# First attention layer of a two-layer block: scores, turns and value products of two row tiles placed one behind the other, and a second buffer for turned probabilities

## The chip, the core and the metric

The program runs on one core of a Trainium2 chip. The core has TensorE for products (with a queue of its own for loading weights), VectorE, ScalarE and GpSimd for elementwise work, and SyncE, which here issues most transfers. The engines run their own instruction streams in order and meet at semaphores. The metric is the time of one execution on the device, in microseconds.

## The reference, cut to what matters

The whole program is a block of two attention layers on one sequence of 512 positions with 1024 features, then a second block (a recurrent branch, a sparse attention branch, a merge). The change is in the first attention layer alone:

```python
def mixer_a(hn, w_in, w_out, q_gain, k_gain, t5_bias):
    proj = hn @ w_in
    qkv = proj[..., :n_qkv].reshape(b, s, N_DIL_GROUPS, 3, N_HEADS, HEAD_DIM)
    gate = proj[..., n_qkv:]
    for g, (window, dilation) in enumerate(DILATED_PAIRS):       # 3 groups, 16 heads of 64
        q = rms_norm(qkv[:, :, g, 0], q_gain[g])
        k = rms_norm(qkv[:, :, g, 1], k_gain[g])
        v = qkv[:, :, g, 2]
        o, lse = dilated_group_attention(q, k, v, t5_bias[...], dilation, reach)
        outs.append(o)
        lses.append(lse)
    alpha = jax.nn.softmax(jnp.stack(lses), axis=0)
    y = jnp.sum(alpha[..., None] * jnp.stack(outs), axis=0)
    y = y.reshape(b, s, BRANCH_WIDTH) * jax.nn.silu(gate)
    return y @ w_out
```

## The kernel before

`dilated_attention` works on eight pairs of heads (p = 0 to 7). While the attention of pair p is computed, the projections of pair p + 1 are computed between its parts. A pair's projection has 13 units u: units 0 to 5 are q and k of the three groups, unit 6 the gate, unit 7 a value block in feature order, units 8 to 11 four value blocks of 256 columns, unit 12 the turning of unit 7 (four transposes). Each of the units 0 to 11 is 24 products: 8 slices of the features, each in three products of rounded high and low parts (`split_product`, lines 321 to 323). Units write two banks in turn, and unit n may start when VectorE has taken unit n - 2 (`project`, semaphore `s_pf`).

For a q or k unit the chain is: ScalarE squares it (1519) and rounds the square (1523); GpSimd forms the rounding's rest (1625); TensorE adds both up over the heads' features in `sum_squares` (1359, 1360), which stands inside the next unit behind 12 of its products; ScalarE makes the inverse norm by a logarithm and an exponential (`inv_norm`, 1507 and 1509); VectorE multiplies unit, gain and norm into `a_qk` (`take`, 1656). Behind the square, ScalarE rounds a block of weights for a later unit (1499) and GpSimd forms its rest (1612).

The attention of a pair has four row tiles t of 128 positions. S t: scores (1405), six or eight products with 64 rows in use; VectorE adds the bias and finds the peak in two passes for each head (`soft_peak`, 1700 and 1702); ScalarE takes four exponentials with their sums (`exps`, 1540); VectorE exchanges peaks and sums between the tiles of different order in eight small operations (`swap`, 1710 and 1711). C and D: shares of the groups. Then `normal` scales the tile's probabilities by the shares (1746), T t turns them on TensorE (1420) into the bank pair `ps_pt`, ScalarE copies one head and VectorE the other into `pt` (`keep_pt`, 1554 and 1754), and A t multiplies them with the values (1436). Behind A3 VectorE multiplies by the gate (`keep_y`, 1766).

The order of it all is written out by hand in two lists, which every engine's code walks through: `PERIOD` for the pairs 0 to 6 and `LAST` for pair 7, in which the out-projection's products (e, f, g, h) stand where the next pair's units do elsewhere. ScalarE and GpSimd do a unit's work at the unit's place; VectorE takes unit i - 1 at the place of unit i.

## Time and profile before

| | us |
|---|---|
| runs, median of 3 | 1609.79 |
| runs, lowest and highest | 1601.22, 1611.5 |
| span of the profiled execution | 1602.5 |
| TensorE busy in that span | 1536.9 (96%) |
| VectorE, ScalarE, GpSimd busy | 807.8, 772.9, 777.1 (50%, 48%, 48%) |
| the seven periods of `PERIOD`, 88 to 594.2 us | 506.2 |
| mean granted clock of TensorE, whole span | 0.987 |

A row of the timeline has the start in us, the duration in us, the engine, the line, the operation, out<-in by the program's names, the shape and a count of merged instructions; in brackets stands how long the engine was idle before, and who ended that. PE is TensorE, DVE VectorE, ACT ScalarE, POOL GpSimd. The matmul rows overlap, since products are pipelined: what a product costs is the distance between two starts, not its duration. A row of the busy times has the stretch, its length, busy us and number of instructions of PE, PEld (weight loading), DVE, ACT and POOL, then the granted clock of TensorE as a share of 2.4 GHz, the share of the transfer engines and GB/s. A row of the waits has who waited for whom: us in total, times, the longest.

### The profile page before, as it was taken

The page shows a single profiled execution, that of the slowest core. Times are in us where ns is not written, and L with a number is a line of the kernel's source. Part 1 is how long each engine was busy: PE and PEld are TensorE (multiplying, and loading weights), DVE is VectorE, ACT ScalarE, POOL GpSimd, SP SyncE. Part 2 cuts the span into 40 slices and gives each one's busy share as a digit, 9 for nine tenths or more (in the row PEclk, how much of TensorE's full clock was granted, in tenths as well). Part 3 has the DMA queues.
Part 4 walks back from the last instruction along what each step waited for, and adds up shares of the span by engine and source line. Part 5 has one row for each costly group of instructions (what it writes and reads, how often), then busy time and mean ns, then how long its engine had stood idle before and what let it go on. Part 6 is the DMA issues. An engine that isn't in the chain of part 4 may idle for free. (4 is left out here: it accounts for less than half of the span.)

```text
span 1602.5 us, 29989 instructions
## 1 busy us (share of the span) xinstructions
PE 1536.9 (96%) x11712; PEld 1236.3 (77%) x11712; DVE 807.8 (50%) x1933; ACT 772.9 (48%) x1558; POOL 777.1 (48%) x474
## 2 busy tenths in 40 slices
PE   7999999999999999999999999999987999999997
PEld 5888787878888787767777776677776886778886
DVE  5145455464545457434445324298437754274545
ACT  4654637364554644455666633356754432352322
POOL 3734436262534443366555544326747651475551
PEclk9999999999999999999999999999979999999998
DMA  6323132232413131355444215132000000323331
GB/s 153 105 83 109 53 97 81 82 97 66 121 40 109 53 96 53 79 153 155 139 140 124 66 54 159 40 73 66 15 29 3 4 17 29 105 80 97 95 98 53
DMA packets 239125, 131.00 MB, mean 82 GB/s; under 512 B 28646, under 2 KB 233518, under 8 KB 238968
## 3 DMA queue, kind: packets, MB, share of 16 engines
q1 hardware_dynamic: 231448, 114.09, 25.6%
q10 hardware_dynamic: 7536, 14.98, 3.1%
q8 instruction: 94, 1.54, 0.4%
q14 instruction: 47, 0.39, 0.1%
HBM read 126.62 MB, written 2.43 MB: 81 GB/s over the span
## 5 line engine op out<-in xcount | busy, mean ns | idle before, releaser
L1612 POOL TENSOR_TENSOR w_low<-a_w_raw,w_high 128x1024 fp32r<-128x1024 f32 x70 | 173.4, 2478 | 56.3 <-ACT w_high L1499 56.3
L321 PE MATMUL a_proj<-h_low,w_high 128*128 128x512 f32 x488 | 196.3, 402 | 1.2 <-POOL h_low L1630 1.2
L323 PE MATMUL a_proj<-h_high,w_high 128*128 128x512 f32 x488 | 192.0, 393 | 0.0
L322 PE MATMUL a_proj<-h_high,w_low 128*128 128x512 f32 x488 | 191.1, 392 | 0.0
L1625 POOL TENSOR_TENSOR a_sq_low<-a_sq,a_sq_high 128x512 fp32r<-128x512 f32 x48 | 63.0, 1312 | 249.9 <-ACT a_sq_high L1523 249.9
L907 POOL TENSOR_TENSOR w_low<-b_w_raw,w_high 128x1024 fp32r<-128x1024 f32 x40 | 100.4, 2512 | 97.1 <-ACT w_high L741 97.1
L321 PE MATMUL b_proj<-h_low,w_high 128*128 128x512 f32 x288 | 116.6, 405 | 1.4 <-POOL h_low L946 0.8
L323 PE MATMUL b_proj<-h_high,w_high 128*128 128x512 f32 x288 | 113.6, 394 | 0.0
L322 PE MATMUL b_proj<-h_high,w_low 128*128 128x512 f32 x288 | 113.5, 394 | 0.0
L321 PEld LDWEIGHTS a_proj<-h_low,w_high 128*128 128x128 f32 x488 | 91.7, 188 | 23.8 <-issue 1.4
L323 PEld LDWEIGHTS a_proj<-h_high,w_high 128*128 128x128 f32 x488 | 91.7, 188 | 20.7
L322 PEld LDWEIGHTS a_proj<-h_high,w_low 128*128 128x128 f32 x488 | 91.8, 188 | 19.0
L1540 ACT ACTIVATE a_probs<-a_probs,a_stat 128x256 f32<-128x256 f32 x128 | 63.2, 495 | 68.3 <-DVE a_stat L1702 68.3
L1499 ACT ACTIVATE w_high<-a_w_raw 128x1024 fp32r<-128x1024 f32 x70 | 73.3, 1047 | 40.5 <-PE a_proj L323 37.5
L1746 DVE TENSOR_SCALAR a_probs<-a_probs,a_share 128x256 f32<-128x256 f32 x128 | 90.4, 768 | 0.3
L1656 DVE SCALAR_TENSOR_TENSOR a_qk<-a_proj,a_gains,a_rn 128x128 f32<-128x128 f32 (+2 forms) x76 | 39.2, 559 | 86.5 <-ACT a_rn L1509 86.1
L3378 POOL TENSOR_TENSOR merge_w_low<-f_wt,merge_w_high 128x1024 fp32r<-128x1024 f32 x22 | 53.5, 2431 | 35.9 <-ACT merge_w_high L3322 35.9
L321 PE MATMUL a_proj<-a_wv_low,h_high 128*128 128x256 f32 x240 | 68.1, 284 | 0.0
L322 PE MATMUL a_proj<-a_wv_high,h_low 128*128 128x256 f32 x240 | 66.9, 279 | 0.0
L323 PE MATMUL a_proj<-a_wv_high,h_high 128*128 128x256 f32 x240 | 66.8, 279 | 0.0
L2328 POOL TENSOR_TENSOR w_low<-sparse_w_raw,w_high 128x1024 fp32r<-128x1024 f32 x15 | 35.8, 2386 | 60.9 <-ACT w_high L2245 58.5
L321 PEld LDWEIGHTS b_proj<-h_low,w_high 128*128 128x128 f32 x288 | 54.6, 190 | 13.4 <-issue 1.4
(554 smaller groups left out, 4187.0 us busy)
## 6 DMA issues: line engine op xcount, KB each, us to landing
a_w_raw<-in_a_w_in_dram SPq DMA_DIRECT2D x78, 512.0 KB, 3.7
b_w_raw<-in_b_w_in_dram SPq DMA_DIRECT2D x30, 512.0 KB, 4.1
b_ada_w<-in_ada_w_dram ACTq DMA_DIRECT2D x24, 512.0 KB, 3.7
f_wt<-in_w_in_dram SPq DMA_DIRECT2D x18, 512.0 KB, 3.6
sparse_w_raw<-in_w_in_dram SPq DMA_DIRECT2D x17, 512.0 KB, 3.6
a_bias<-scr_a SPq DMA_DIRECT2D x32, 128.0 KB
a_w_raw<-in_a_w_out_dram SPq DMA_DIRECT2D x8, 512.0 KB, 4.3
b_w_raw<-in_b_w_out_dram SPq DMA_DIRECT2D x8, 512.0 KB, 4.2
```

What stands on the lines that cost most here:

```text
L321: nc.tensor.matmul(out, lh, rl, start=first, stop=False)
L322: nc.tensor.matmul(out, ll, rh, start=False, stop=False)
L323: return nc.tensor.matmul(out, lh, rh, start=False, stop=last)
L907: nc.gpsimd.tensor_tensor(low(slot_of(b)), raw[:, n % RAW, :, :], high(slot_of(b)), ALU.subtract).then_inc(s_wl, 1)
L1499: nc.scalar.activation(high(slot_of(b)), raw[:, n % RAW, :, :], ACT.Copy).then_inc(s_wh, 1)
L1540: nc.scalar.activation(e, e, ACT.Exp, scale=-1.0, bias=stat[:, own, part, t, h, 0:1], accum_out=stat[:, own, part, t, h, 1:2]).then_inc(s_ ...
L1612: nc.gpsimd.tensor_tensor(low(slot_of(b)), raw[:, n % RAW, :, :], high(slot_of(b)), ALU.subtract).then_inc(s_wl, 1)
L1625: nc.gpsimd.tensor_tensor(sql[:, :], sq[:, u % 2, :], sqh[:, :], ALU.subtract).then_inc(s_sql, 1)
L1656: return nc.vector.scalar_tensor_tensor(out=out, in0=x, scalar=col(gains, u), in1=r, op0=ALU.mult, op1=ALU.mult)
L1746: nc.vector.tensor_scalar(e, e, share[:, part, t, h:h + 1], None, ALU.mult).then_inc(s_pn, 1)
L2328: nc.gpsimd.tensor_tensor(wl[:, slot(u), :, :], wraw[:, u % RAW, :, :], wh[:, slot(u), :, :], ALU.subtract).then_inc(s_wl, 1)
L3378: nc.gpsimd.tensor_tensor(low(b)[:, :, :], raw_of(b), high(b)[:, :, :], ALU.subtract).then_inc(s_wl, 1)
```

## The change

In `PERIOD` the scores, turns and value products of two tiles stand directly behind each other, and the scaling of the tiles 1 to 3 gets places of its own (N). The turns T0 and T1 move behind unit 6, A2 and A3 behind unit 12. In `LAST` only the scores are put in pairs. So that two tiles can be in work at once, the odd tiles' scores go to the bank pair that was used for turns alone, the odd tiles' turns (pairs 0 to 6) to the bank pair of the scores, and `pt` has two buffers. The exchange of tile t now stands behind the pass over tile t + 1 for all pairs. The waits are renumbered to fit.

```diff
--- before.py
+++ after.py
@@ -1166,10 +1166,10 @@
     w_out = I["a_w_out"][0].rearrange("(k p) n -> p k n", p=P)
     X, Y, HH, HL = T.X0, T.Y, T.HH, T.HL
 
-    PERIOD = [("S", 0), ("u", 0), ("S", 1), ("u", 1), ("S", 2), ("u", 2), ("S", 3), ("u", 3), ("C", 0), ("u", 4), ("D", 0), ("u", 5),
-              ("T", 0), ("u", 6), ("A", 0), ("T", 1), ("u", 7), ("A", 1), ("T", 2), ("u", 8), ("u", 9), ("A", 2), ("T", 3),
-              ("u", 10), ("u", 11), ("A", 3), ("u", 12)]
-    LAST = [("S", 0), ("e", 0), ("S", 1), ("e", 1), ("S", 2), ("e", 2), ("S", 3), ("e", 3), ("e", 4), ("C", 0), ("e", 5),
+    PERIOD = [("S", 0), ("S", 1), ("u", 0), ("u", 1), ("S", 2), ("S", 3), ("u", 2), ("u", 3), ("C", 0), ("u", 4), ("D", 0), ("u", 5),
+              ("N", 1), ("u", 6), ("T", 0), ("T", 1), ("N", 2), ("u", 7), ("N", 3), ("u", 8), ("A", 0), ("A", 1), ("T", 2), ("T", 3),
+              ("u", 9), ("u", 10), ("u", 11), ("u", 12), ("A", 2), ("A", 3)]
+    LAST = [("S", 0), ("S", 1), ("e", 0), ("e", 1), ("S", 2), ("S", 3), ("e", 2), ("e", 3), ("e", 4), ("C", 0), ("e", 5),
             ("D", 0), ("e", 6), ("f", 0), ("f", 1), ("f", 2), ("f", 3), ("T", 0), ("f", 4), ("f", 5), ("A", 0), ("T", 1),
             ("f", 6), ("g", 0), ("A", 1), ("T", 2), ("g", 1), ("g", 2), ("A", 2), ("T", 3), ("g", 3), ("g", 4), ("A", 3),
             ("g", 5), ("g", 6), ("h", 0), ("h", 1), ("e", 7), ("f", 7), ("g", 7)] + [("h", k) for k in range(2, KT)]
@@ -1273,7 +1273,7 @@
         rn = sb("rn", [P, SEQ])
         bias = sb("bias", [P, 2, BIAS])
         probs = sb("probs", [P, 4, 2, 2 * WIN])
-        pt = sb("pt", [P, 2, 4, P])
+        pt = sb("pt", [P, 2, 2, 4, P])
         stat = sb("stat", [P, 2, 2, 4, 2, 2])
         lead, diff = sb("lead", [P, LINE]), sb("diff", [P, 2, LINE])
         share = sb("share", [P, 2, 4, 2])
@@ -1291,6 +1291,9 @@
         proj_bank = lambda n: banks[bank_of(n)]
         out_bank = lambda m: banks[m % 6]
         bank_user = lambda n: max([m for m in range(max(0, n - UNITS), n) if bank_of(m) == bank_of(n)])
+        paired = lambda p: p < PAIRS - 1
+        score_tile = lambda t: ps_pt if t % 2 else ps_s
+        turn_tile = lambda p, t: ps_s if paired(p) and t % 2 else ps_pt
 
         s_small = sem("gains_in")
         s_w = [sem(f"w{i}") for i in range(RAW)]
@@ -1396,13 +1399,17 @@
 
                 if t == 0:
                     pe.wait_ge(s_pf, UNITS * p + NQK if p else IN_SCORES)
-                if p or t:
-                    pe.wait_ge(s_l2, 2 * (4 * p + t))
+                if t >= 2:
+                    pe.wait_ge(s_l2, 2 * (4 * p + t - 1))
+                elif p:
+                    pe.wait_ge(s_pa, 4 * p - t)
+                    pe.wait_ge(s_pbk, 4 * p - t)
+                tile = score_tile(t)
                 near = [(0, t * P, WIN)] if t < 3 else [(0, t * P, P), (P, 0, P)]
                 for g, c0, k0, w in [(0, *n) for n in near] + [(1, WIN, t * P, P), (2, WIN + P, t * P, P)]:
                     for h in range(2):
                         hp = slice(h * HD, (h + 1) * HD)
-                        mm = nc.tensor.matmul(ps_s[:, h, c0:c0 + w], qk[hp, p % 2, 2 * g, t * P:(t + 1) * P],
+                        mm = nc.tensor.matmul(tile[:, h, c0:c0 + w], qk[hp, p % 2, 2 * g, t * P:(t + 1) * P],
                                               qk[hp, p % 2, 2 * g + 1, k0:k0 + w], start=True, stop=True)
                         if g == 2:
                             mm.then_inc(s_S, 1)
@@ -1410,14 +1417,16 @@
             def turn(p, t):
 
                 n = 4 * p + t
-                if n == 0:
-                    pe.wait_ge(s_pf, IN_TURNED)
+                tile = turn_tile(p, t)
+                if t == 0:
+                    pe.wait_ge(s_l2, 8 * (p + 1))
+                back = 2 if paired(p) else 1
                 for h in range(2):
                     pe.wait_ge(s_pn, 4 * n + 2 * h + 2)
-                    if n:
-                        pe.wait_ge(s_pbk if h else s_pa, n)
+                    if t >= back:
+                        pe.wait_ge(s_pbk if h else s_pa, n - back + 1)
                     for c in range(4):
-                        mm = nc.tensor.transpose(ps_pt[:, h, c * P:(c + 1) * P], probs[:, t, h, c * P:(c + 1) * P], T.ident)
+                        mm = nc.tensor.transpose(tile[:, h, c * P:(c + 1) * P], probs[:, t, h, c * P:(c + 1) * P], T.ident)
                     mm.then_inc(s_Tb if h else s_Ta, 1)
 
             def apply_v(p, t):
@@ -1432,7 +1441,8 @@
                     for h in range(2):
                         o = ps_o[h * HD:(h + 1) * HD, :]
                         into = by_time(o)[:, :, 3 - t, :] if g == 0 else o[:, (3 - t) * P:(4 - t) * P]
-                        moving = pt[:, h, c, :].rearrange("p (c j) -> p c j", c=4) if g == 0 else pt[:, h, c, :]
+                        turned = pt[:, t % 2, h, c, :]
+                        moving = turned.rearrange("p (c j) -> p c j", c=4) if g == 0 else turned
                         mm = nc.tensor.matmul(into, vt[:, p % 2, tile, g * P + h * HD:g * P + (h + 1) * HD], moving,
                                               start=(t == 0 and c == 0), stop=(t == 3 and c == 3), skip_group_check=True)
                 mm.then_inc(s_O, 1)
@@ -1549,9 +1559,10 @@
 
                 n = 4 * p + t
                 act.wait_ge(s_Ta, n + 1)
-                if n:
-                    act.wait_ge(s_O, n)
-                nc.scalar.activation(pt[:, 0, :, :], ps_pt[:, 0, :].rearrange("p (c n) -> p c n", n=P), ACT.Copy).then_inc(s_pa, 1)
+                if n >= 2:
+                    act.wait_ge(s_O, n - 1)
+                nc.scalar.activation(pt[:, t % 2, 0, :, :], turn_tile(p, t)[:, 0, :].rearrange("p (c n) -> p c n", n=P),
+                                     ACT.Copy).then_inc(s_pa, 1)
 
             def y_high(k):
                 act.wait_ge(s_y, k + 1)
@@ -1697,9 +1708,9 @@
                     tiles = bias[:, h, 0:4 * P].rearrange("p (n j) -> p n j", n=4)
                     near = tiles[:, 2:0:-1, :] if t == 0 else tiles[:, 0::3, :] if t == 3 else tiles[:, 0:2, :]
                     two = lambda a: a.rearrange("p (n j) -> p n j", n=2)
-                    nc.vector.tensor_tensor_reduce(two(probs[:, t, h, 0:WIN]), two(ps_s[:, h, 0:WIN]), near, -1.0, HUGE,
+                    nc.vector.tensor_tensor_reduce(two(probs[:, t, h, 0:WIN]), two(score_tile(t)[:, h, 0:WIN]), near, -1.0, HUGE,
                                                    ALU.add, ALU.min, stat[:, own, 0, t, h, 0:1])
-                    nc.vector.tensor_tensor_reduce(probs[:, t, h, WIN:], ps_s[:, h, WIN:], bias[:, h, 4 * P:], -1.0, HUGE,
+                    nc.vector.tensor_tensor_reduce(probs[:, t, h, WIN:], score_tile(t)[:, h, WIN:], bias[:, h, 4 * P:], -1.0, HUGE,
                                                    ALU.add, ALU.min, stat[:, own, 1, t, h, 0:1]).then_inc(s_l2, 1)
 
             def swap(p, t):
@@ -1749,9 +1760,9 @@
 
                 n = 4 * p + t
                 dve.wait_ge(s_Tb, n + 1)
-                if n:
-                    dve.wait_ge(s_O, n)
-                nc.vector.tensor_copy(pt[:, 1, :, :], ps_pt[:, 1, :].rearrange("p (c n) -> p c n", n=P)).then_inc(s_pbk, 1)
+                if n >= 2:
+                    dve.wait_ge(s_O, n - 1)
+                nc.vector.tensor_copy(pt[:, t % 2, 1, :, :], turn_tile(p, t)[:, 1, :].rearrange("p (c n) -> p c n", n=P)).then_inc(s_pbk, 1)
 
             def split_low(b):
 
@@ -1771,9 +1782,7 @@
                 for kind, i in plan(p):
                     if kind == "S":
                         soft_peak(p, i)
-                        if p < PAIRS - 1 and i < 3:
-                            swap(p, i)
-                        if p == PAIRS - 1 and i:
+                        if i:
                             swap(p, i - 1)
                     elif kind == "C":
                         swap(p, 3)
@@ -1783,8 +1792,10 @@
                         normal(p, 0)
                     elif kind == "u" and i:
                         take(p + 1, i - 1)
+                    elif kind == "N":
+                        normal(p, i)
                     elif kind == "T":
-                        if i < 3:
+                        if not paired(p) and i < 3:
                             normal(p, i + 1)
                         keep_pt(p, i)
                         if p == PAIRS - 1 and i in (0, 2):
```

On ScalarE, at the third scores of a period (`a_rn` the inverse norm, `a_sq` a unit's square, `a_probs` exponentials, four for each tile). Before:

```order
L1499 ACTIVATE w_high<-a_w_raw 128x1024
L1540 ACTIVATE a_probs,a_stat<-a_probs,a_stat 128x256 x4
L1507 ACTIVATE a_rn<-a_ss,eps 128x512
L1509 ACTIVATE a_rn<-a_rn 128x512
L1519 ACTIVATE a_sq<-a_proj 128x512
```

After:

```order
L1509 ACTIVATE w_high<-a_w_raw 128x1024
L1550 ACTIVATE a_probs,a_stat<-a_probs,a_stat 128x256 x8
L1517 ACTIVATE a_rn<-a_ss,eps 128x512
L1519 ACTIVATE a_rn<-a_rn 128x512
L1529 ACTIVATE a_sq<-a_proj 128x512
```

Behind the weights of unit 1 there were four exponentials and then the norm of unit 1; now there are eight, those of tiles 2 and 3.

On VectorE, behind the pass over the third scores (L1710 and L1711, afterwards L1721 and L1722, are the exchange; L1656, L1667 the take of a unit; L1700 and L1702, L1711 and L1713 the pass). Before, from the second half of the exchange on:

```order
L1710 TENSOR_TENSOR a_stat<-a_stat 32x4
L1711 TENSOR_TENSOR a_stat<-a_stat 32x4
L1710 TENSOR_TENSOR a_stat<-a_stat 32x4
L1711 TENSOR_TENSOR a_stat<-a_stat 32x4
L1656 SCALAR_TENSOR_TENSOR a_qk<-a_proj,a_gains,a_rn 128x4x112
L1656 SCALAR_TENSOR_TENSOR a_qk<-a_proj,a_gains,a_rn 128x4x16
L1700 ISA a_probs,a_stat<-a_scores,a_bias 128x256
L1700 ISA a_stat 128x1
```

After:

```order
L1721 TENSOR_TENSOR a_stat<-a_stat 32x4
L1722 TENSOR_TENSOR a_stat<-a_stat 32x4
L1721 TENSOR_TENSOR a_stat<-a_stat 32x4
L1722 TENSOR_TENSOR a_stat<-a_stat 32x4
L1711 ISA a_probs,a_stat<-a_turned,a_bias 128x256
L1711 ISA a_stat 128x1
L1713 ISA a_probs,a_stat<-a_turned,a_bias 128x256
L1713 ISA a_stat 128x1
```

Behind the exchange stood the take of unit 1, now stands the pass over the fourth scores (behind it another exchange follows, and only then that take).

On TensorE, where one pair ends and the next begins (L321 to L323 are products of units, L1383 or L1386 unit 12, L1436 or L1446 value products, L1405 or L1412 scores). Before:

```order
L323 MATMUL a_proj<-a_wv_high,h_high 128x256
L1436 MATMUL a_o<-a_pt,a_v 64x4x32 x4
L1436 MATMUL a_o<-a_pt,a_v 64x128 x4
L1383 MATMUL a_proj<-consts,a_v_feature_major 128x128 x4
L1405 MATMUL a_scores<-a_qk 128x256 x2
L1405 MATMUL a_scores<-a_qk 128x128 x4
L321 MATMUL a_proj<-h_low,w_high 128x512
```

After:

```order
L323 MATMUL a_proj<-a_wv_high,h_high 128x256
L1386 MATMUL a_proj<-consts,a_v_feature_major 128x128 x4
L1446 MATMUL a_o<-a_pt,a_v 64x4x32 x4
L1446 MATMUL a_o<-a_pt,a_v 64x128 x4
L1446 MATMUL a_o<-a_pt,a_v 64x4x32 x4
L1446 MATMUL a_o<-a_pt,a_v 64x128 x4
L1412 MATMUL a_scores<-a_qk 128x256 x2
L1412 MATMUL a_scores<-a_qk 128x128 x4
L1412 MATMUL a_turned<-a_qk 128x256 x2
L1412 MATMUL a_turned<-a_qk 128x128 x4
L321 MATMUL a_proj<-h_low,w_high 128x512
```

A2 and A3 now stand behind unit 12, and S0 and S1 directly behind them, ahead of the next unit.

## Rows read from the trace of the kernel before

Pair 1's attention and the projections of pair 2 are in work from 160.4 us on; the rows of the timeline are from there if nothing else is said.

**Rows 1.** Busy time by engine in the seven periods of pairs 0 to 6.

```profile
88.00:594.20 506.20, 506.20 (x3167) 419.16 (x3165) 253.53 (x777) 260.61 (x518) 221.96 (x112) 1.00 0.29 83
```

**Rows 2.** The waits of TensorE in the attention layer, 84 to 640 us.

```profile
PE a_proj L321 <- POOL h_low L1630: 1.2, 1, 1.2
PE a_scores L1405 <- DVE a_stat L1702: 0.2, 1, 0.2
```

**Rows 3.** Timeline of TensorE around the second scores of pair 1.

```profile
161.79 0.39 PE L322 MATMUL a_proj<-h_high,w_low 128*128 128x512 f32 x1
...
166.83 0.40 PE L323 MATMUL a_proj<-h_high,w_high 128*128 128x512 f32 x1
167.16 1.15 PE L1405 MATMUL a_scores<-a_qk 64*128 64x256 f32 x12
168.23 0.50 PE L321 MATMUL a_proj<-h_low,w_high 128*128 128x512 f32 x1
168.57 0.40 PE L322 MATMUL a_proj<-h_high,w_low 128*128 128x512 f32 x1
```

**Rows 4.** Timeline of TensorE, value product and turns of pair 1.

```profile
207.97 0.40 PE L323 MATMUL a_proj<-h_high,w_high 128*128 128x512 f32 x1
208.29 1.09 PE L1436 MATMUL a_o<-a_pt,a_v 128*64 128x128 f32 x16
209.32 1.09 PE L1420 MATMUL a_turned<-consts,a_probs 128*128 128x128 f32 x8
210.17 0.48 PE L321 MATMUL a_proj<-h_low,w_high 128*128 128x512 f32 x1
210.49 0.40 PE L322 MATMUL a_proj<-h_high,w_low 128*128 128x512 f32 x1
```

**Rows 5.** Timeline of TensorE, where units 3 and 4 touch.

```profile
191.40 0.40 PE L323 MATMUL a_proj<-h_high,w_high 128*128 128x512 f32 x1
191.78 0.50 PE L1359 MATMUL a_ss<-a_sq_low,pair_ones_r 128*128 128x512 f32 x1
192.12 0.40 PE L1360 MATMUL a_ss<-a_sq_high,pair_ones_r 128*128 128x512 f32 x1
```

**Rows 6.** Timeline of ScalarE behind the second scores of pair 1.

```profile
167.26 0.60 ACT L1519 ACTIVATE a_sq<-a_proj 128x512 f32<-128x512 f32 x1 [2.59 <-PE a_proj L323]
...
169.38 0.49 ACT L1540 ACTIVATE a_probs<-a_probs,a_stat 128x256 f32<-128x256 f32 x1
...
171.77 0.69 ACT L1507 ACTIVATE a_rn<-a_ss,eps 128x512 f32<-128x512 f32 x1 [0.33 <-PE a_ss L1360]
```

**Rows 7.** Timeline of GpSimd at the same place.

```profile
168.60 1.30 POOL L1625 TENSOR_TENSOR a_sq_low<-a_sq,a_sq_high 128x512 fp32r<-128x512 f32 x1 [21.34 <-ACT a_sq_high L1523]
169.86 2.40 POOL L1612 TENSOR_TENSOR w_low<-a_w_raw,w_high 128x1024 fp32r<-128x1024 f32 x1
```

**Rows 8.** Timeline of VectorE there, and its next take.

```profile
168.47 0.42 DVE L1700 CUSTOM_DVE_ANT_0 a_probs<-a_scores,a_bias 128x256 f32<-128x256 f32 x1 [2.76 <-PE a_scores L1405]
...
171.47 0.81 DVE L1710 TENSOR_TENSOR a_stat<-a_stat 32x4 f32<-32x4 f32 x1 [1.53 <-ACT a_probs L1540]
172.20 0.15 DVE L1711 TENSOR_TENSOR a_stat<-a_stat 32x4 f32<-32x4 f32 x1
...
173.17 1.13 DVE L1656 SCALAR_TENSOR_TENSOR a_qk<-a_proj,a_gains,a_rn 128x128 f32<-128x128 f32 x4
...
180.44 1.17 DVE L1656 SCALAR_TENSOR_TENSOR a_qk<-a_proj,a_gains,a_rn 128x448 f32<-128x448 f32 x2
```

**Rows 9.** Timeline of TensorE behind two idle times later in the program.

```profile
1074.49 0.49 PE L2191 MATMUL s_scores<-s_kt,sparse_in 64*128 64x128 f32 x4 [1.58 <-DVE s_peak L2430]
...
1419.97 0.49 PE L321 MATMUL f_p<-f_y_low,merge_w_high 128*128 128x512 f32 x1 [2.52 <-POOL f_y_low L3397]
```

**Rows 10.** Busy time and clock (third number from the end) behind these two.

```profile
1075.50:1078.90 3.40, 3.40 (x11) 2.65 (x10) 3.23 (x12) 0.94 (x3) 0.00 (x0) 0.51 0.41 124
1420.30:1423.60 3.30, 3.30 (x9) 2.62 (x8) 3.27 (x3) 0.55 (x1) 3.30 (x2) 0.50 0.08 13
```

## Prediction

> **What bounds the kernel now.** The busy times of the stretch come first: the seven periods in which the change acts, one for each of the pairs 0 to 6, last 506.2 us together, 72.3 each, and TensorE is busy in all of it [rows 1]. VectorE, ScalarE and GpSimd are each about half busy there, so none is the bound; but their order decides when TensorE gets a free bank. The waits of TensorE over the whole attention layer are two, 1.2 and 0.2 us, both in the last pair [rows 2]. So a period can only be shortened by work or gaps taken from TensorE's own stream, and any new wait of TensorE is added in full. The timeline of TensorE shows those gaps: products of a unit start 0.229 us apart (161.79 to 166.83 are 22 of them), but the scores start 0.33 behind the last of them, and the second product behind the scores starts 0.34 behind the first [rows 3]. That is 0.10 on the way in and 0.11 on the way out; the scores themselves take 1.07.
>
> **The merged groups (a gain).** A period has now eight groups of attention products between stretches of projection, afterwards four. Four groups merged away save at most 4 x (0.10 + 0.11) = 0.84. Where a value product stands before turns, 16 products of which each loads 64 columns take 1.03, and the way in is 0.32 - 0.23 = 0.09, the way out 0.32 - 0.23 = 0.09 [rows 4]. Three of the five changes of kind inside a group stay; two go, at about 0.1 each, as estimated from that way in. So 0.84 + 0.2 = 1.04, call it -1.0 a period. Bounds: -0.6 (the seam inside a merged group costs half of what it replaces) and -1.3 (a score group also loses its first exposed load). The Trainium skill, page TensorEngine Tiling (Array Packing), section Key Properties, says that a change of tiling mode drains TensorE. A period has 16 such changes now and 7 afterwards; at 0.10 each that would make -0.9. The rows show that turns, which are in the same 128x128 form as the projection, pay 0.09 on the way out too, so the mode is not all of it.
>
> **Sums of squares (a loss).** Unit u+1 holds, after 12 of its 24 products, the sum of squares of unit u, which waits for a square, a rounding and a GpSimd difference. Where a group of attention stands between the two units it is on time; where the units touch it is not: it starts 0.38 behind the product before it and its second half 0.34 behind the first, against 0.23 each [rows 5]: 0.26. Units touch at two such places now (3 to 4, 4 to 5). Afterwards also 0 to 1 and 5 to 6: +0.5. A fifth, 2 to 3, is covered by the next term.
>
> **The bank of unit 3 (the main term).** Units 0 to 12 write two banks in turn, so unit 3 waits until VectorE has taken unit 1. What is in front of that take changes. Count from the start of the third score product group (S2) and use the second group of a period of before, which has the same work behind it: it starts at 167.16 [rows 3].
>
> ScalarE squares unit 1 at +0.10; GpSimd's difference of squares starts at +1.44 and its weight difference at +2.70, lasting 2.40, so to +5.10 [rows 6, 7].
>
> VectorE's first pass over S2 starts at +1.31 and ends near +2.8 [rows 8]. Then comes the exchange of the sums of tile 1, eight tiny operations. In the period of before its first operation started at 171.47, while GpSimd's weight difference ran until 172.26, and took 0.81; the second started at 172.20 and took 0.15, and VectorE's next work started at 173.17, 0.91 behind GpSimd's end [rows 7, 8]. So: exchange over at 5.10 + 0.91 = +6.0.
>
> Only now VectorE passes over S3. ScalarE's exponentials follow 0.91 behind the start of a pass (168.47 to 169.38) and four of them take 2.06 (to 171.44, where the idle time of 0.33 ahead of the logarithm begins): until 6.0 + 0.91 + 2.06 = +9.0. Now they stand ahead of the logarithm for unit 1.
>
> Logarithm to take is 1.40 (171.77 to 173.17), and the take of unit 1 lasts 1.17 [rows 6, 8]: bank free at 9.0 + 1.40 + 1.17 = +11.5.
>
> TensorE: two score groups 2 x 1.07, 0.11 out, 24 products of 0.229 (5.50) and the sum of squares 0.46: it wants the bank at +8.2.
>
> The wait is 11.5 - 8.2 = +3.3 a period, and 0.1 for the exposed load behind it. Upper bound 3.6 (the 0.3 that the seam between S2 and S3 may save, since TensorE comes sooner). Lower bound 1.1: if the exchange were not held by GpSimd it would take about 1.0 (seven of its operations take 172.20 to 173.17) and end at +3.8, not +6.0. Behind this nothing more goes late: GpSimd finds unit 2 squared before unit 3 is half through; the take of unit 2 keeps the spacing it has now.
>
> The Trainium skill, page SBUF — State Buffer, section Who interferes with whom, says that a VectorE instruction with two SBUF inputs and a GpSimd one that reads SBUF exclude each other, whichever issues first. If the exchange came first, by +2.70, its first operation alone would be free and the other seven would wait for a GpSimd instruction that ends 0.15 later: 3.4 for 3.3.
>
> **TensorE's clock.** In this stretch the granted clock is 1.00, the 2.4 GHz level [rows 1]. Later in the program TensorE stood idle for 2.52 us; then the granted clock was 0.50 (1.2 GHz) for 3.3 us. Behind an idle time of 1.58 it fell too, to 0.51 for 3.4 us [rows 9, 10]. At half the clock 3.3 us of products do the work of 1.65: +1.6 per wait of 3.3. Bounds 0 (no fall) and 1.7.
>
> **What costs nothing.** T0 and T1 now stand behind unit 6, about 6 us later, while the scalings of tiles 0 and 1 keep their place on VectorE, so they are early. The scaling of tile 2 stands ahead of the gate's take, for which unit 8 waits; unit 7 (5.50) covers it, with two copies, four scalings and one hold by GpSimd of at most 2.40 in it. I estimate half a us to spare; if that cover is gone, up to 1.0 a period. The second copy of the turned tile costs memory only, and takes a wait from ScalarE and VectorE, not from TensorE. No transfer moves in its queue; the next pair's bias, released by the pass over S3, comes some 4 us later, with most of a period in hand.
>
> **The last pair.** Its first out-product no longer waits 1.2 us for GpSimd [rows 2], because A2, A3, S0 and S1 (four groups of about 1) stand between it and the projection's end. Two merged scores give 0.4. Against it, later rows of y stand behind exponentials as before, while the products come sooner; I give back 0.6. -1.0, bounds -1.6 and +0.5.
>
> **Sum.** A period: -1.0 + 0.5 + 3.3 + 0.1 + 1.6 = +4.5. Seven: +31.5; less 1.0: +30.5. The profiled execution has a span of 1602.5, so 1633; the median of the runs is 7.3 above that, at 1609.8, and on that scale 1640 (ratio 1.019).
>
> **Rivals.**
>
> *The wait comes, the clock stays*, or falls while TensorE is idle anyway: 7 x 2.9 - 1.0 = +19, 1629. For it: the fall came 0.3 us behind the end of the one idle time and 1.0 behind the other, so where it lies is partly chance. Against: both were shorter than 3.3 and both were followed by it.
>
> *GpSimd does not hold the exchange.* Then the wait is 1.1, shorter than both idle times of [rows 9], and I leave the clock up: 7 x (1.1 + 0.1 + 0.5 - 1.0) - 1.0 = +4, 1614. Against it: the row of 0.81.
>
> *Not slower: the bank is free in time.* This happens if unit 1's take is done by +8.2, as when the exponentials of tile 3 do not stand ahead of its logarithm. Then 7 x (-1.0 + 0.5) - 1.0 = -4.5, 1605, within 1%. More than 1% faster would need -2.1 a period, beyond every gap in [rows 3, 4]. The order on ScalarE speaks against it.
>
> *A second wait.* The gate's take for unit 8 is also late, by up to 1.0: 7 more, 1647.
>
> **How the numbers follow.** Chances: forecast 0.60, clock stays 0.18, no hold 0.08, in time 0.06, second wait 0.08. The predicted time is that of the first, 1640. The range leaves out the two quick cases (0.14) and takes in the others with their bounds: below: wait and clock as in the forecast but the clock's fall partly inside the idle time, and the program nearer to the profiled span than to the median; above: a wait of 3.6, merging worth 0.6, and the second wait: 1620 to 1653. One per cent, 16 us, is about what a measurement of this kernel can tell from no change. Slower by over 1% are the forecast, the second wait and most of "clock stays": 0.82. Within 1%: 0.15. Faster: 0.03.
>
> **What would show it.** In the changed profile TensorE waits at unit 3 for the VectorE take of unit 1, seven times, longest 3.0 to 3.6, and VectorE's first exchange operation of tile 1 lasts about 2.3. The clock in the middle of each period is below 1.00. A period is 75 to 77.5 us. The wait for GpSimd in the last pair is gone. Wrong would be: no such wait, a wait of about 1 us (no hold), or a wait at another place such as unit 8.

## Result and profile after

| | before | after |
|---|---|---|
| median of 5 runs each, us | 1606.81 | 1630.6 |
| lowest and highest, us | 1601.22, 1611.5 | 1627.04, 1631.06 |
| ratio, 95% interval | | 1.0154 [1.0135, 1.0173] |
| span of the profiled execution, us | 1602.5 | 1627.8 |
| the seven periods, from the first scores of pair 0 to those of pair 7, us | 506.1 | 532.1 |

The change makes the kernel 1.5% slower. The forecast was 1640 with a range of 1620 to 1653, slower by over 1% with a chance of 0.82. Of the 25.3 us by which the span grew, the seven periods hold 26.0. They last 76.25, 74.85, 74.87, 77.45, 76.41, 74.79 and 77.48 us, against 72.3 each. The work ahead of the first scores is 1.9 shorter, the last pair 1.3 shorter, the rest of the program, whose code is the same, 2.5 longer. Such a spread in unchanged code is found between all profiled executions here: the first scores start anywhere from 84.1 to 88.1 us.

The waits of TensorE, 84 to 670 us, in the kernel after (engine, line, who is waited for: us in total, times, the longest):

```profile
PE a_proj L321 <- DVE a_qk L1667: 21.9, 7, 3.1
PE a_proj L321 <- POOL h_low L1641: 1.0, 1, 1.0
```

Against [rows 2] a new wait stands there, once in each period, for VectorE's take of a unit. The wait for GpSimd in the last pair is not the one of [rows 2]. That one stood before the first out-product (596.55, the pair's first scores at 594.20) and is gone; this one stands 12.3 us behind the first scores (618.29), before a product with later rows of y:

```profile
630.55 0.50 PE L321 MATMUL a_proj<-h_low,w_high 128*128 128x512 f32 x1 [0.98 <-POOL h_low L1641]
```

The busy times of 84 to 594.2 us answer to [rows 1]:

```profile
84.00:594.20 510.20, 487.83 (x2971) 405.94 (x2970) 244.84 (x758) 253.65 (x510) 216.11 (x110) 0.98 0.27 78
```

TensorE is now idle for 22.4 us of this stretch (510.20 less 487.83), and its granted clock is 0.98 on the mean.

Timeline of TensorE in the first period of after, around the third and fourth scores (a row that merges several instructions has their count behind the x):

```profile
100.08 1.15 PE L1412 MATMUL a_scores<-a_qk 64*128 64x256 f32 x12
101.06 1.06 PE L1412 MATMUL a_turned<-a_qk 64*128 64x128 f32 x16
102.05 0.50 PE L321 MATMUL a_proj<-h_low,w_high 128*128 128x512 f32 x1
...
107.91 0.40 PE L323 MATMUL a_proj<-h_high,w_high 128*128 128x512 f32 x1
111.45 0.79 PE L321 MATMUL a_proj<-h_low,w_high 128*128 128x512 f32 x1 [3.15 <-DVE a_qk L1667]
```

The two groups of scores take 1.97 together (100.08 to 102.05), where two single ones took 2 x 1.07 and two ways in and out [rows 3]. The wait of 3.15 ends at the first product of unit 3. It is counted from the end of the product before; from start to start it is 3.54 (107.91 to 111.45), 3.31 more than the usual 0.229. Timeline of VectorE in between:

```profile
101.37 0.42 DVE L1711 CUSTOM_DVE_ANT_0 a_probs<-a_scores,a_bias 128x256 f32<-128x256 f32 x1 [1.43 <-PE a_scores L1412]
...
102.87 2.33 DVE L1721 TENSOR_TENSOR a_stat<-a_stat 32x4 f32<-32x4 f32 x1
105.13 0.15 DVE L1722 TENSOR_TENSOR a_stat<-a_stat 32x4 f32<-32x4 f32 x1
...
106.08 0.42 DVE L1711 CUSTOM_DVE_ANT_1 a_probs<-a_turned,a_bias 128x256 f32<-128x256 f32 x1
...
110.24 1.16 DVE L1667 SCALAR_TENSOR_TENSOR a_qk<-a_proj,a_gains,a_rn 128x448 f32<-128x448 f32 x2 [1.66 <-ACT a_rn L1519]
```

The same stretch of ScalarE:

```profile
106.90 0.51 ACT L1550 ACTIVATE a_probs<-a_probs,a_stat 128x256 f32<-128x256 f32 x1 [2.53 <-DVE a_stat L1713]
...
108.88 0.66 ACT L1517 ACTIVATE a_rn<-a_ss,eps 128x512 f32<-128x512 f32 x1
```

And of GpSimd:

```profile
102.78 2.41 POOL L1623 TENSOR_TENSOR w_low<-a_w_raw,w_high 128x1024 fp32r<-128x1024 f32 x1
```

Read from below: the take of unit 1 (110.24) waits for the inverse norm, whose logarithm (108.88) stands behind the four exponentials of tile 3. Those began at 106.90, when VectorE's pass over the fourth scores (from 106.08) gave them their first row. The pass stood behind the exchange of tile 1, whose first operation of 32x4 took 2.33 us, from 102.87 to 105.20. GpSimd's weight difference ran from 102.78 to 105.19. The same kind of operation takes 0.15 in the next row.

TensorE's clock behind the wait, in the periods 1, 4, 5, 7 and 3 (granted clock third from the end):

```profile
111.40:115.00 3.60, 3.54 (x9) 2.85 (x10) 0.00 (x1) 0.90 (x1) 3.57 (x2) 0.57 0.00 0
337.40:342.70 5.30, 5.28 (x12) 4.13 (x13) 0.00 (x0) 0.86 (x1) 3.60 (x2) 0.50 0.07 21
414.80:418.50 3.70, 3.63 (x9) 2.92 (x10) 0.01 (x1) 0.91 (x1) 3.60 (x2) 0.54 0.02 4
566.20:571.40 5.20, 5.20 (x13) 4.04 (x14) 0.00 (x0) 0.72 (x1) 3.46 (x2) 0.50 0.09 27
262.50:266.00 3.50, 3.45 (x15) 2.85 (x16) 0.00 (x0) 0.90 (x1) 3.48 (x2) 1.00 0.00 0
```

Behind the same wait the clock falls to 1.2 GHz in four periods (1, 4, 5, 7) and stays at 2.4 GHz in three (a figure such as 0.57 is the mean of a stretch with both levels). In the three a period is 74.79 to 74.87; the four are 1.4, 2.6, 1.6 and 2.6 longer, 8.2 in all.

### The profile page after: what moved, and what is told of

Same layout as the page of the kernel before. It is cut to its first block and busy times, and to the rows that moved or that the text cites. A ratio compares the mean times of both kernels' runs of the same rounds, so it can differ in the third digit from the quotient of the medians.

```text
span 1627.8 us, 29967 instructions
## 1 busy us (share of the span) xinstructions
PE 1539.9 (95%) x11712; PEld 1243.2 (76%) x11712; DVE 809.8 (50%) x1933; ACT 771.7 (47%) x1558; POOL 776.5 (48%) x474
## 5 line engine op out<-in xcount | busy, mean ns | idle before, releaser
L321 PE MATMUL a_proj<-h_low,w_high 128*128 128x512 f32 x488 | 198.3, 406 | 22.9 <-DVE a_qk L1667 21.9
L323 PE MATMUL a_proj<-h_high,w_high 128*128 128x512 f32 x488 | 194.7, 399 | 0.0
L321 PEld LDWEIGHTS a_proj<-h_low,w_high 128*128 128x128 f32 x488 | 93.6, 192 | 48.0 <-DVE a_qk L1667 24.9
L1667 DVE SCALAR_TENSOR_TENSOR a_qk<-a_proj,a_gains,a_rn 128x128 f32<-128x128 f32 (+2 forms) x76 | 39.2, 560 | 167.6 <-ACT a_rn L1519 167.6
L321 PE MATMUL b_proj<-h_low,w_high 128*128 128x512 f32 x288 | 117.1, 407 | 1.4 <-POOL h_low L946 0.8
L323 PE MATMUL b_proj<-h_high,w_high 128*128 128x512 f32 x288 | 113.8, 395 | 0.0
L323 PEld LDWEIGHTS a_proj<-h_high,w_high 128*128 128x128 f32 x488 | 93.5, 192 | 21.3
L1757 DVE TENSOR_SCALAR a_probs<-a_probs,a_share 128x256 f32<-128x256 f32 x128 | 85.3, 729 | 0.3
L321 PE MATMUL a_proj<-a_wv_low,h_high 128*128 128x256 f32 x240 | 67.7, 282 | 0.0
L323 PE MATMUL a_proj<-a_wv_high,h_high 128*128 128x256 f32 x240 | 67.1, 280 | 0.0
L321 PEld LDWEIGHTS b_proj<-h_low,w_high 128*128 128x128 f32 x288 | 54.7, 190 | 13.3 <-issue 1.6
```

Of the source, the lines that this page charges most:

```text
L321: nc.tensor.matmul(out, lh, rl, start=first, stop=False)
L323: return nc.tensor.matmul(out, lh, rh, start=False, stop=last)
L1667: return nc.vector.scalar_tensor_tensor(out=out, in0=x, scalar=col(gains, u), in1=r, op0=ALU.mult, op1=ALU.mult)
L1757: nc.vector.tensor_scalar(e, e, share[:, part, t, h:h + 1], None, ALU.mult).then_inc(s_pn, 1)
```

## Experiments

The theory: the bank of unit 3 comes late for two reasons, one in VectorE's order (an exchange, held by GpSimd, ahead of the pass over the fourth scores) and one in ScalarE's (the exponentials of tile 3 ahead of unit 1's logarithm). The rivals: the hold by GpSimd has no part in it; or one of the two orders alone decides.

**late_s3.** ScalarE and VectorE both go through `late(p)`: the work on the fourth scores behind unit 2's; the exchange of tile 2 next to that of tile 3.

```diff
+    LATE = [x for x in PERIOD if x != ("S", 3)]
+    LATE.insert(LATE.index(("u", 2)) + 1, ("S", 3))
+    late = lambda p: LATE if p < PAIRS - 1 else LAST
...
-                for kind, i in plan(p):
+                for kind, i in late(p):
...
-                        if i:
+                        if i and not (paired(p) and i == 3):
                             swap(p, i - 1)
                     elif kind == "C":
+                        if paired(p):
+                            swap(p, 2)
```

> The changed kernel, with TensorE's order untouched, but on ScalarE and VectorE the fourth tile's work (the pass over S3 and its exponentials) moved behind unit 2, that is behind the norm and the take of unit 1; the exchange of tile 2 moves to the place C. My theory (unit 3's bank is late because the pass over S3, the held exchange and four exponentials stand ahead of the take of unit 1) expects the wait of 3.1 us in each of the seven periods to fall to under 0.5, no fall of the clock in the periods, and a period of 71.5 to 72.0 for 72.3 before the change and 74.8 to 77.5 with it: 1594 to 1600 on the profiled span, ratio 0.994 to 0.998. Rival A (the wait comes from GpSimd or from the products themselves, and the order on the two engines only shifts it) expects the wait at unit 3 or a new one of over 1 us at unit 4. Rival B (merging the groups gains nothing, and touching units cost 0.26 each) expects no wait, but a period of 72.8 or more, ratio over 1.000.

Measured: 1624.34, ratio 1.0124 [1.0108, 1.0141], a period 75.12 to 75.24. The wait before unit 3 is gone. Two others have come in its place in the first three periods, before the units 5 and 6. Timeline of TensorE in late_s3:

```profile
123.01 0.50 PE L321 MATMUL a_proj<-h_low,w_high 128*128 128x512 f32 x1 [1.87 <-DVE a_qk L1670]
130.86 0.50 PE L321 MATMUL a_proj<-h_low,w_high 128*128 128x512 f32 x1 [1.60 <-DVE a_qk L1670]
```

In the periods 4 to 7 only the first of them is there, and the clock falls behind it. Timeline of TensorE in period 4:

```profile
348.59 0.50 PE L321 MATMUL a_proj<-h_low,w_high 128*128 128x512 f32 x1 [1.86 <-DVE a_qk L1670]
...
350.53 0.63 PE L322 MATMUL a_proj<-h_high,w_low 128*128 128x512 f32 x1
350.96 0.63 PE L323 MATMUL a_proj<-h_high,w_high 128*128 128x512 f32 x1
```

Starts lie 0.43 apart there, for 0.23, from 349.86 to 353.09. The slower products fill the time in which TensorE waits in the first three periods, so a period is no longer than theirs. Timeline of VectorE in late_s3, ahead of the two waits of period 1:

```profile
116.19 1.28 DVE L1725 TENSOR_TENSOR a_stat<-a_stat 32x4 f32<-32x4 f32 x1
117.50 2.33 DVE L1724 TENSOR_TENSOR a_stat<-a_stat 32x4 f32<-32x4 f32 x1
...
122.20 0.75 DVE L1670 SCALAR_TENSOR_TENSOR a_qk<-a_proj,a_gains,a_rn 128x512 f32<-128x512 f32 x1 [1.53 <-ACT a_rn L1522]
...
124.77 5.38 DVE L1760 TENSOR_SCALAR a_probs<-a_probs,a_share 128x256 f32<-128x256 f32 x4
130.07 0.74 DVE L1670 SCALAR_TENSOR_TENSOR a_qk<-a_proj,a_gains,a_rn 128x512 f32<-128x512 f32 x1
```

Of GpSimd:

```profile
116.16 1.30 POOL L1639 TENSOR_TENSOR a_sq_low<-a_sq,a_sq_high 128x512 fp32r<-128x512 f32 x1 [2.57 <-ACT a_sq_high L1536]
117.42 2.39 POOL L1626 TENSOR_TENSOR w_low<-a_w_raw,w_high 128x1024 fp32r<-128x1024 f32 x1
```

And of ScalarE:

```profile
120.70 0.23 ACT L1559 ACTIVATE a_diff<-a_diff 128x32 f32<-128x32 f32 x1 [3.67 <-DVE a_diff L1739]
120.84 0.67 ACT L1520 ACTIVATE a_rn<-a_ss,eps 128x512 f32<-128x512 f32 x1
```

Sixteen exchange operations now stand in a row, and two long operations of GpSimd meet the twelfth and the thirteenth: 1.28 and 2.33 us, each ending with GpSimd's (117.47 and 117.46; 119.83 and 119.81). ScalarE's next norm is queued behind an exponential that needs the exchange, so unit 3's take comes at 122.20. Unit 4's take (130.07) stands behind the scaling of tile 0, whose four operations take 5.38 us beside two more long differences of GpSimd (124.66 to 129.47). In the kernel before the same four took 1.14, with no operation of GpSimd beside them but for their last 0.09 (the next starts at 196.65):

```profile
195.60 1.14 DVE L1746 TENSOR_SCALAR a_probs<-a_probs,a_share 128x256 f32<-128x256 f32 x4
```

The slowest single one took 2.50 in late_s3. So both new waits have a hold by GpSimd in their chain. The expectation failed because it looked at one bank only: 3.1 us of wait at one unit became 3.5 at two others. It also said that the clock would not fall. That a hold by GpSimd costs time is borne out, in other places.

**exp_late.** Only ScalarE's order is changed (`late(p)` in its loop).

> The changed kernel with ScalarE's order alone altered: the exponentials of tile 3 stand behind the norm of unit 1; VectorE keeps the order of the change. My theory expects the norm early, but VectorE's take still stands behind the held exchange, the pass over S3 and the next exchange (until about 8.5 us behind the start of S2, and 1.2 more for the take, against 8.0 when TensorE wants the bank): the wait falls from 3.1 to 1.3 to 1.7. If the exponentials ahead of the norm were all that matters, as one rival of the prediction had it, the wait would be under 0.3. If GpSimd's hold is all that matters, it stays at about 3.1.

Measured: 1608.47 in one run, span 1606.7, a period 73.13 to 73.22, the wait 1.5. Timeline of VectorE in exp_late:

```profile
175.85 2.30 DVE L1724 TENSOR_TENSOR a_stat<-a_stat 32x4 f32<-32x4 f32 x1
...
179.03 0.42 DVE L1714 CUSTOM_DVE_ANT_1 a_probs<-a_turned,a_bias 128x256 f32<-128x256 f32 x1
...
180.53 0.15 DVE L1724 TENSOR_TENSOR a_stat<-a_stat 32x4 f32<-32x4 f32 x1
...
181.55 1.17 DVE L1670 SCALAR_TENSOR_TENSOR a_qk<-a_proj,a_gains,a_rn 128x448 f32<-128x448 f32 x2
```

Of GpSimd there:

```profile
175.73 2.40 POOL L1626 TENSOR_TENSOR w_low<-a_w_raw,w_high 128x1024 fp32r<-128x1024 f32 x1
```

The inverse norm was ready at 179.89; the take starts at 181.55, right behind two exchanges and a pass on VectorE's own queue, with no idle time ahead of it. Taking the second reason away alone is worth 1.6 of the 3.1.

**swap_behind.** Only VectorE's order is changed: the exchange of tile 1 behind the pass over the fourth scores.

```diff
-                        if i:
+                        if i and not (paired(p) and i == 2):
+                            if paired(p) and i == 3:
+                                swap(p, 1)
                             swap(p, i - 1)
```

> The changed kernel with one edit on VectorE: the exchange of tile 1 stands behind the pass over S3 instead of ahead of it. So GpSimd's weight difference can hold the exchange no longer than before, but no longer ahead of the pass and the exponentials. My theory gives the held exchange 2.2 us of the wait: the pass over S3 would start at +2.8, its exponentials end at +6.3, the norm follows, and the take ends at +8.8 to 9.0 against 8.0: the wait falls from 3.1 to 0.6 to 1.0, and the clock no longer falls in the periods. If the hold by GpSimd does not matter, the wait stays at about 3.1. If the hold only moves and delays the take from its new place as long, the wait is 2 or more.

Measured: 1601.84 in one run, span 1600.1, a period 72.14 to 72.21, the wait 0.5, a little under the 0.6 to 1.0 expected. Timeline of VectorE in swap_behind:

```profile
176.52 0.93 DVE L1721 TENSOR_TENSOR a_stat<-a_stat 32x4 f32<-32x4 f32 x1
...
179.85 1.16 DVE L1667 SCALAR_TENSOR_TENSOR a_qk<-a_proj,a_gains,a_rn 128x448 f32<-128x448 f32 x2 [0.52 <-ACT a_rn L1519]
```

Of GpSimd there:

```profile
175.02 2.41 POOL L1623 TENSOR_TENSOR w_low<-a_w_raw,w_high 128x1024 fp32r<-128x1024 f32 x1
```

The passes run under GpSimd's operation at their usual pace, and only the last 0.93 of it holds the exchange (ends 177.45 and 177.43). Here the take waits 0.52 for ScalarE, so the other reason is what is left. Taking the hold away saves 2.6 of the 3.1. This and the 1.6 of exp_late overlap: the two reasons lie side by side on two engines, and each gain is what the other leaves.

**both.** The two edits together.

> Both delays of unit 1's take gone at once: DVE's exchange of tile 1 stands behind the pass over S3, and the exponentials of tile 3 stand behind unit 2's row in ACT's order. If the wait before unit 3 is the sum of the exchange that GpSimd holds and of the late logarithm, it is 0.2 us or less in each period (0.5 with the first edit alone, 1.5 with the second alone), a period is 71.6 to 71.9 us, and the ratio to the kernel before is 0.995 to 0.998. If some other step is late next, a wait of 0.4 or more stands elsewhere and a period is 72.1 or more (ratio 0.999 or over).

Measured: 1599.18, ratio 0.9968 [0.9951, 0.9984], a period 71.69 to 71.75, and in the seven periods no wait of TensorE for VectorE that shows beside its products. The change with these two orders is no slower than before; by the interval it is 0.2 to 0.5% faster. What is left shows in the timeline of the weight loads (PEld) of this kernel, where a late take costs less than its wait, since loads run ahead. The two loads for a take cost 0.54 together in a period (from start to start in period 3: 0.31 and 0.23 more than usual). In period 2:

```profile
180.52 0.19 PEld L321 LDWEIGHTS a_proj<-h_low,w_high 128*128 128x128 f32 x1 [0.45 <-DVE a_qk L1670]
186.78 0.19 PEld L321 LDWEIGHTS a_proj<-h_low,w_high 128*128 128x128 f32 x1 [0.39 <-DVE a_qk L1670]
...
195.83 0.19 PEld L1365 LDWEIGHTS a_ss<-a_sq_low,pair_ones_r 128*128 128x128 f32 x1 [0.36 <-POOL a_sq_low L1639]
```

**warm.** The changed kernel, with 12 products whose result nobody uses in the wait before unit 3, into the bank pair of the scores.

```diff
+                        if i == 3:
+                            pe.wait_ge(s_l2, 2 * (4 * p + 3))
+                            for _ in range(12):
+                                nc.tensor.matmul(ps_s[:, 0, :], T.pair_ones_r, HH[:, 0, :], start=True, stop=True)
```

> The changed kernel with 12 products of 512 columns that are used nowhere, put on TensorE ahead of unit 3 (into the bank of the third scores, once those are read), so that TensorE works for 2.75 us of the wait of 3.1. The wait for the take itself is not touched. My theory (idle time of about 3 us lets the clock fall in part of the periods, which cost 8.2 us in the profiled execution over the seven) expects every period at 74.8 to 74.9, no clock under 1.00 in them, and 6 to 9 us less than the changed kernel: ratio 1.009 to 1.012 to the kernel before. The rival (the long periods of 76.3 to 77.5 have another cause than the idle time) expects them still there and a ratio of about 1.015.

Measured: 1624.66, ratio 1.0121 [1.0102, 1.014]; a period 74.75 to 74.83, all seven alike, clock 1.00 in all of them. Timeline of TensorE in warm:

```profile
108.57 2.89 PE L1490 MATMUL a_scores<-h_high,pair_ones_r 128*128 128x512 f32 x12
...
111.88 0.51 PE L321 MATMUL a_proj<-h_low,w_high 128*128 128x512 f32 x1 [0.42 <-DVE a_qk L1671]
```

The unit begins no sooner, but no fall follows: the seven periods take 523.6 instead of 532.1. So the clock's part is 8 us, and it comes from TensorE's idling, not from the work that waits. The span is only 4.5 shorter, since the rest of the program was 4.0 longer in this execution; so the ratio stands at the upper end of what was expected.

**scores_only2** (swap_behind with turns and value products one at a time, in the order of before) and **turns_only** (the changed kernel with the scores one at a time) divide the gain.

> The scores in pairs and the exchange of tile 1 behind the pass over S3, but turns and value products one at a time as before (only 2 of the 6 merged pairs of a period). If each merged pair is worth about 0.2 us and unit 6 no longer touches unit 5, a period is 72.5 to 72.8 us, against 72.17 with all six merged; if the merging of turns and value products is worth nothing, it is 71.9.

> Scores one at a time as before, turns and value products in pairs (4 of the 6 merged pairs). The exchange of tile 1 does not meet GpSimd's long multiplication, so no wait of over 0.3 us stands before unit 3, and TensorE's clock does not fall. If each merged pair is worth 0.2 us, a period is 71.6 to 71.9 us, and the span 1597 to 1600. If the wait comes from the pairs of turns and not from those of the scores, it stays at 3 us and a period is 75.

Measured: scores_only2 1606.54 in one run, a period 72.48, of it a wait of 0.48; turns_only 1598.77 in one run, a period 71.95, no wait. Each has one touching place more than before (0.25 in the one, 0.22 in the other, from start to start). The wait of 0.48 costs 0.76 from start to start. So the two merged pairs of scores are worth 72.30 + 0.25 + 0.76 - 72.48 = 0.83, the four of turns and value products 72.30 + 0.22 - 71.95 = 0.57. In turns_only the exchange is held as well, against what I wrote, and it costs nothing. Its timeline of VectorE:

```profile
168.34 2.31 DVE L1721 TENSOR_TENSOR a_stat<-a_stat 32x4 f32<-32x4 f32 x1
...
171.53 1.13 DVE L1667 SCALAR_TENSOR_TENSOR a_qk<-a_proj,a_gains,a_rn 128x128 f32<-128x128 f32 x4
```

Behind it stands the take, no second pass and no second exchange. It is the pair of scores that turns a hold into a wait.

**both_k4.** Additionally, the sums of squares inside units 1 and 6 one step (three products) later.

```diff
-                        if p and k == 3 and 1 <= u <= NQK:
+                        if p and k == (4 if u in (1, 6) else 3) and 1 <= u <= NQK:
                             sum_squares(p, u - 1)
```

> As both, with the sums of squares that follow units 0 and 5 one step later inside units 1 and 6, so that their squares are there. If the 0.26 us per place that the prediction adds for them is a weight load exposed by a late square, this gives it back: 71.1 to 71.4 us per period, ratio 0.993 to 0.996, and TensorE's weight loads for the sums of squares wait 14 times instead of 28. If one step (0.7 us) later is not late enough, or the load would be exposed at any place, a period is as in both (71.6 to 71.9).

Measured: 1593.71, ratio 0.9937 [0.9921, 0.9953], a period 71.14 to 71.20. Two places give back 0.58, 0.29 each. It is the fastest of all kernels here, 0.5 to 0.8% faster than before by the interval. The weight loads waited for squares 8 times by the list of waits, not 14: those inside unit 5 are left, and those inside unit 4 wait 0.18 at most.

**before_k4** (the kernel before) and **both_k4_all** (both) have the step later in every unit: `k == 4` in that line.

> The kernel before, with the sums of squares one step later inside every unit. If the cost of a touching unit is the weight load that waits for GpSimd's squares, its two places in each period (inside units 4 and 5) give back 0.26 us each: a period goes from 72.30 to 71.8 us, 14 waits of TensorE's weight loads for the squares go, and the ratio is 0.997 to 0.9985. If a place costs nothing where it was already there, a period stays at 72.3 and the ratio is 1.000.

> As both_k4, with the step later at the other units too. Against both_k4 (71.17 us per period) one wait of 0.41 us before a weight load is left, in unit 5; if it goes, a period is 70.9 us, and the ratio to the kernel before is 0.991 to 0.994. The difference to the kernel before_k4, which has the same places without the pairs, is then what the pairs alone are worth: 6 merged groups, 0.9 to 1.1 us a period. If the later sum of squares delays a bank instead, a new wait stands before units 5 or 6, and a period is 71.2 or more.

For before_k4 neither value came, and both_k4_all took the way that was named as the other one, a later bank. before_k4: 1606.08, ratio 1.0014 [0.9999, 1.0029], a period 72.67. both_k4_all: 1603.46, ratio 0.9999 [0.9983, 1.0014], a period 72.43 to 72.51, 1.3 more than both_k4. The waits for squares are gone in both. Timeline of the weight loads of before_k4:

```profile
187.42 0.19 PEld L321 LDWEIGHTS a_proj<-h_low,w_high 128*128 128x128 f32 x1 [0.56 <-DVE a_qk L1656]
193.83 0.19 PEld L321 LDWEIGHTS a_proj<-h_low,w_high 128*128 128x128 f32 x1 [0.56 <-DVE a_qk L1656]
```

Of both_k4_all:

```profile
181.95 0.19 PEld L321 LDWEIGHTS a_proj<-h_low,w_high 128*128 128x128 f32 x1 [0.99 <-DVE a_qk L1670]
188.37 0.19 PEld L321 LDWEIGHTS a_proj<-h_low,w_high 128*128 128x128 f32 x1 [0.58 <-DVE a_qk L1670]
```

These are the first products of the units 3 and 4; those of 5 and 6 wait 0.58 each as well.

The sum of squares of a unit leads to its norm, its take and so the bank of the unit after next. One step later is 0.7 us later for that bank. Where no attention group stands in between, the wait only changes its name: in before_k4 a unit's distance to the next goes from 6.23 (with the exposed load) to 6.40. In both_k4 the two moved places are those where the third scores, or turns, stand ahead of the unit that needs the bank; there the step was free. The difference of both_k4_all and before_k4 doesn't give the worth of the pairs, as I had written, because their bank waits are not the same.

## Why the prediction was right

The time lies in the range and the sign is right. The terms, for one period, counted from start to start (a quiet period of after, one whose clock does not fall, is 74.84):

| term | forecast | measured |
|---|---|---|
| merged groups | -1.0 | -1.42 (what is left) |
| two more touching places | +0.5 | +0.56 |
| wait for the bank of unit 3 | +3.3 | +3.28 |
| exposed load behind it | +0.1 | +0.12 |
| clock | +1.6 | +1.17 (8.2 in seven) |
| sum | +4.5 | +3.7 |

The wait in period 2 of after:

```profile
184.18 0.39 PE L323 MATMUL a_proj<-h_high,w_high 128*128 128x512 f32 x1
187.69 0.51 PE L321 MATMUL a_proj<-h_low,w_high 128*128 128x512 f32 x1 [3.12 <-DVE a_qk L1667]
188.04 0.40 PE L322 MATMUL a_proj<-h_high,w_low 128*128 128x512 f32 x1
```

3.51 between the first two starts and 0.35 between the next two, for 0.229 each, make 3.28 and 0.12. The 3.12 in brackets, counted from the end of the product before, is less than TensorE's stream lost.

**Merged groups.** This term was too small, and it came out beyond its own bound of -1.3: 74.84 - 72.30 - 3.28 - 0.12 - 0.56 = -1.42, and -1.40 by the two kernels that divide it. Read group by group in period 3, the four scores with their ways in and out take 5.04 before and 4.24 after; turns, value products and unit 12 take 8.77 and 8.00. That is 1.57 less, of which about 0.15 is lost again, spread over the units. The step that was too small is the one for the scores: a merged pair saves 0.40, not 0.21. Besides the ways in and out, each group in a pair takes 0.98 for 1.07; I had that only as a bound. Turns and value products save 0.14 a pair by turns_only.

**Touching places.** The waits of the weight loads for GpSimd's squares in after, 84 to 600 us:

```profile
PEld a_ss L1362 <- POOL a_sq_low L1636: 12.1, 28, 0.5
```

They are 28, twice the 14 of two places in seven periods. Three of the four places of a period cost about 0.25 each in after, the one inside unit 6 0.33; the two that both_k4 takes away give 0.29 each. Right.

**The bank of unit 3.** The chain held at each step, counted from the third scores (100.08): end of GpSimd's difference 5.1 forecast and 5.1 measured, exchange over 6.0 and 6.0, exponentials over 9.0 and 8.8, bank free 11.5 and 11.3, TensorE wants it 8.2 and 8.1 (0.229 behind the start at 107.91), unit 3 begins at 11.4.

The Trainium skill says on its page SBUF — State Buffer, section Who interferes with whom, that a VectorE instruction with two SBUF inputs and a GpSimd one that reads SBUF exclude each other. The traces agree in six places of the kernels above: 2.33, 1.28, 2.33, 2.30, 0.93 and 2.31 us for an operation of 0.15, each ending within 0.03 us of GpSimd's.

**The clock.** This term was too large. [rows 9, 10] show a fall behind 1.58 and behind 2.52 us of idling, and I took it as certain behind 3.3. It came in four of seven periods whose wait is the same to 0.03 us, and lasted 3 to 5 us. late_s3 has the same mixture behind 1.87 us of idling (four of seven), exp_late no fall in seven behind 1.5. What decides it in a period is left open. So the sign that I gave, a clock below 1.00 in the middle of each period, is seen in four, and the periods are 74.8 to 77.5 us for the 75 to 77.5 that I named.

**What costs nothing.** T0, T1, the gate's take and unit 8 show no wait in after: right. The second copy of the turned tile and the bias transfers cost nothing either.

**The last pair.** The total is right (-1.3 for -1.0), its parts are not. The first out-product no longer waits, as forecast: 1.28 from start to start. The two merged pairs of scores save 0.80, not 0.4. The seams ahead of the third and fourth scores, 0.40 and 0.31 before because of VectorE's pass, for 0.10 elsewhere, are gone: 0.51, which I had not counted. Against it stands the later wait for GpSimd, in kind the one for which I gave back 0.6; it costs 1.25 (629.18 to 630.55 and the load behind it). Together -1.34. So the sign that no wait for GpSimd would be left in the last pair was wrong.

**Scale.** The median of before was 1609.79 with three runs and is 1606.81 with five, and I added the forecast to the former. That is 3 of the 9.4 us by which 1640 is too high. The periods account for 5.5 (31.5 for 26.0), about half of it from the merging and half from the clock; 0.9 is left.

**Rivals.** "GpSimd does not hold the exchange" falls by the row of 2.33. "A second wait" fell too. "The clock stays" came half true. The condition that I gave for "the bank is free in time" was wrong: it names the exponentials alone, and exp_late shows 1.5 of wait without them ahead of the logarithm, because the held exchange, a pass and a second exchange stand before the take on VectorE. It takes both orders.

## What to carry to other kernels

Merging short groups of another kind on a saturated TensorE does pay (here 1.4 us of 72), but two groups side by side also deliver two portions of work to the engines behind, and what those engines must do for a bank in between gets stuck behind the second portion. When pairing work on one engine, write out the queues of the others from the pair to the next bank that is wanted, and put the small operations that another engine can hold behind the ones that it can't. Shift a short dependent product to a later step only where something else stands between it and the unit that needs its result; otherwise the wait moves to the bank, at a higher price.

## What the runs showed of the hardware

- An idle time of TensorE of 3.1 us was followed by half the clock in four of seven cases, two of them for over 5 us; with 12 unused products in the gap it was followed by none in seven. Behind 1.87 us (late_s3) the clock fell in four of seven cases too, about 1.3 us behind the end of the idling; behind 1.5 us (exp_late) in none of seven.
- A VectorE operation of 0.15 us with two operands in SBUF lasted as long as GpSimd's running one, up to 2.33 us, also when it came in the middle; the passes over scores in PSUM did not slow down beside it.
- Four VectorE scalings of 128x256 took 1.14 us in before, almost clear of GpSimd, and 5.38 in late_s3 beside two long operations of GpSimd, the slowest single one 2.50.
- A weight load that waits for its data costs TensorE's stream about 0.16 us less than it waits, from start to start: 0.41 costs 0.25, 0.57 costs 0.41, 0.94 costs 0.79, 3.56 costs 3.40. The idle time in the rows of TensorE itself shows nothing of the short ones and 3.12 of the last.
